# Split weight tiles 16 bytes later in their rooms: activations stand 48 in place of 64 bytes off them modulo 128

## The chip, the cores and the metric

The kernel runs on one core of one Trainium2 chip. Its time is the device time of one execution, in microseconds; three runs of the kernel before gave 1188.04, 1191.52 and 1197.49 us. The profile is of one further execution.

## The reference

Three transformer layers on one sequence of 256 tokens with a width of 1024, all in float32. Each `@` below is a matrix product with weights that are read once from memory.

```python
# layer 0
x = x + conformer_conv(rms_norm(x), w_pw1 [1024x2048], w_dw [31 taps], w_pw2 [1024x1024])
x = x + memory_cross_attention(rms_norm(x), mem, w_q, w_k, w_v, w_o)      # each 1024x1024
x = x + (silu(h @ w_gate) * (h @ w_up)) @ w_down      # h = rms_norm(x), 1024x2816, 2816x1024
# layer 1
k, v = shared_kv(x, w_k, w_v)
x = x + diff_attention(rms_norm(x), k, v, w_q, w_o)
x = x + memory_cross_attention(...)
x = x + swiglu(...)                                   # 1024x2816 twice, 2816x1024
x = rms_norm(x)
# last layer (hybrid)
proj = rms_norm(x) @ w_in                             # 1024x1816
o = three NSA branches and a sliding window attention on proj
x = x + rms_norm(o @ w_out)                           # 1024x1024
x = x + rms_norm(gated_conv_ffn(rms_norm(x), w_up [1024x5632], conv of width 3, w_down [2816x1024]))
```

## The kernel before, in words

**Tiles.** All weights are cut into tiles of 1024 x 256 (8 chunks of 128 rows, 256 columns), 1 MB each, in the order in which the stages use them. The activations lie transposed in on-chip memory: 128 partitions, and for each chunk of 128 features one row of 256 tokens (`Hhi`, `Hlo`, `FH`, `FL`, `KVr` and others, float32).

**Splitting.** Most products are made from split operands. A weight tile arrives by DMA in `raw[j]` (j is 0 or 1, two buffers in turn). ACT copies it in two halves to `whi[j]`, which has the shorter type float32r (`split`, lines 1004 and 1007); DVE then takes `raw[j] - whi[j]` and writes it to `wlo[j]`, the low part (`lower`, lines 1451 and 1456). The activations are split in the same way into a high and a low tensor. For each chunk the function `three` issues three matmuls into the same sum: high by high (line 491), low activations by high weights (492), high activations by low weights (493). Each matmul has its own weight load, which the profile shows as PEld, and which runs while the matmul before it streams.

**Turned and not.** In `matmul(dst, w, x)` the first operand, 128 columns, is loaded into the array, and the second, 256 columns, is streamed. Mostly the loaded one is a slice of `whi` or `wlo` and the streamed one a chunk of activations. In a few stages, turned ones, it is the reverse: activations are loaded and `whi` or `wlo` streamed, so that the result has the tokens on the partitions. Among them are the values of the attention (`diffv`), the last part of the input projection, the output projection `wout` and the last down projection `down2`. The profile's names list the streamed operand first: `acc<-Hhi,whi` streams `Hhi` and loads `whi`, `acc<-whi,FH` streams `whi` and loads `FH`.

**Order.** Every engine has its program written out by hand, and semaphores link them. A tile's chain is: SP issues the load of `raw[j]` once `wlo[j]` of the tile before in this buffer is written (`lo_dve`); ACT waits for the load and for the matmuls of the tile two before (`tile_done`); DVE waits for ACT; PE waits for DVE (`tile_in`), and for a free accumulator (`acc_free`). Between the splits ACT and DVE do the elementwise work of the stage. Memory keys and values (`memk`, `memv`, `memk1`) are made from `raw` directly in full float32, without a split (lines 507 and 527). In `wout` the four weight tiles have places of their own (`out_weights`): the first two use `whi` and `wlo`, the third `Hhi` and `Hlo`, the fourth parts of `KVr`.

**Places.** `sb` allocates on-chip memory from the front, one tensor after the other; a tensor's bytes are those of one partition. `raw`, `whi` and `wlo` are three pairs of 8192 bytes. Behind them lies `apart`, which nothing reads or writes: 176 x 4 = 704 bytes, or 5 x 128 + 64. Everything from `X` on to the constants `cst` (`Hhi`, `Hlo`, `H2`, `MEM`, `FH`, `FL`, `KVr`, `MKV`, `A`) has a size that is a multiple of 1024 bytes, and chunks of 1024 bytes. By this order of allocation `raw`, `whi` and `wlo` stand at 0 modulo 128 and all the activations at 64 modulo 128; every slice that a matmul takes of them starts at a multiple of 512 bytes from the tensor's start. `Hhi` and `FH`, and `KVr` and `FH`, which meet in `wout`, stand 0 apart modulo 128.

Of the kernel before, what the change touches and what calls it, by code (L numbers as in the profile page):

```python
# [7 lines left out]
F32R = mybir.dt.float32r  # L8
# [8 lines left out]
P = 128  # L17
# [6 lines left out]
KC = 8  # L24
MB = 256
# [134 lines left out]
def build(nc, weights, consts, x_in, mem_in, positions, out):  # L160
    ctx = ExitStack()
    with ctx:
        def sb(name, shape, dt=F32, where=ctx):
            return where.enter_context(nc.sbuf_tensor(name, shape, dt))
# [3 lines left out]


        raw = [sb(f"raw{j}", [P, KC, MB]) for j in range(2)]  # L170
        whi = [sb(f"whi{j}", [P, KC, MB], F32R) for j in range(2)]
        wlo = [sb(f"wlo{j}", [P, KC, MB], F32R) for j in range(2)]
        sb("apart", [P, 176])
        X = sb("X", [P, DC, S])
        SQ = sb("SQ", [P, DC, S])
# [2243 lines left out]
```

## Time and profile before

| what | us |
|---|---|
| median of three runs | 1191.52 |
| lowest and highest | 1188.04, 1197.49 |
| the profiled execution's own time | 1196.01 |
| its span, first to last instruction | 1194.2 |
| PE busy (matmuls) | 1144.7 |
| PE weight loads busy | 1088.0 |
| DVE busy | 876.8 |
| ACT busy | 612.3 |
| POOL busy | 64.3 |
| read from memory | 194.12 MB |

PE is the matmul engine, PEld its weight load, which overlaps with the matmuls; DVE and ACT are the two elementwise engines; SP issues most DMAs. The matmuls are pipelined: one lasts nearly 300 ns in the records, but the next starts long before it ends, so several are in flight, and a matmul's cost is the distance from one start to the next. A count of instructions in a window takes in those that were already running at its left edge. The mean granted clock of TensorE is 0.99 of full speed. Some rows stand in a window, given as start:end in us from the start of the span.

### The profile page before, as it was taken

What the parts mean: (1) busy time and instruction counts of PE and PEld (TensorE: products, weight loads), DVE (VectorE), ACT (ScalarE), POOL (GpSimd) and SP (SyncE); (2) the same over time, 40 slices, a digit from 0 to 9 for tenths busy, and PEclk for the clock granted to TensorE, in tenths of its full rate; (3) what the DMA queues carried; (4) which work ended last, traced back from release to release, by engine and by line L of the source; (5) the groups of instructions that cost most, each with busy time, mean ns of one, the idle gap of its engine ahead of it and who ended that gap; (6) DMA issues with size and microseconds to landing.
All of it is one profiled execution on the core that took longest, in us unless ns stands there. A gap on an engine that the chain in (4) does not pass through costs nothing.

```text
span 1194.2 us, 24046 instructions
## 1 busy us (share of the span) xinstructions
PE 1144.7 (96%) x9142; PEld 1088.0 (91%) x9142; DVE 876.8 (73%) x1480; ACT 612.3 (51%) x1072; POOL 64.3 (5%) x53
## 2 busy tenths in 40 slices
PE   9999999999999999998999999999979799999997
PEld 8988898999999999778989999999967599999997
DVE  6999886676666687556768666657897857999954
ACT  6754555544445544344445444454455745666542
POOL 0677000000000000000000000000000000000000
PEclk9999999999999999999999999999989989999999
DMA  8554443355555656124524555565553213455562
GB/s 286 177 189 164 141 162 121 128 191 190 196 188 199 212 188 226 63 72 162 207 70 170 189 189 195 177 212 196 210 181 107 71 41 124 172 183 198 181 212 106
DMA packets 32008, 198.42 MB, mean 166 GB/s; under 512 B 3776, under 2 KB 6080, under 8 KB 9024
## 3 DMA queue, kind: packets, MB, share of 16 engines
q1 hardware_dynamic: 29440, 193.09, 46.8%
q10 hardware_dynamic: 2496, 4.33, 1.1%
q8 instruction: 51, 0.84, 0.3%
q14 instruction: 21, 0.17, 0.0%
HBM read 194.12 MB, written 1.05 MB: 163 GB/s over the span
## 4 chain that ended last, share of the span: by engine, by line
PE 74%; DVE 17%; ACT 3%; issue 3%; DMA 1%; ACTq 0%; DVEq 0%; SPq 0%
PE acc L491 21%; PE acc L492 20%; PE acc L493 20%; DVE sc L1923 4%; PE acc L507 2%; DVE wlo L1456 2%; PE acc L774 2%; DMA raw<-weights 1%; PE acc L527 1%; DVE wlo L1451 1%; PE sc L738 1%; PE st L642 1%; PE tp L763 1%; ACT whi L1004 1%; DVE mx L1833 1%
## 5 line engine op out<-in xcount | busy, mean ns | idle before, releaser
L491 PE MATMUL acc<-Hhi,whi 128*128 128x256 f32 x1368 | 384.3, 281 | 5.3 <-DVE wlo L1456 5.2
L492 PE MATMUL acc<-Hlo,whi 128*128 128x256 f32 x1368 | 381.1, 279 | 0.0
L493 PE MATMUL acc<-Hhi,wlo 128*128 128x256 f32 x1368 | 381.1, 279 | 0.0
L1004 ACT ACTIVATE whi<-raw 128x1024 fp32r<-128x1024 f32 x160 | 169.4, 1059 | 335.1 <-PE acc L493 304.3
L1451 DVE TENSOR_TENSOR wlo<-raw,whi 128x1024 fp32r<-128x1024 f32 (+1 forms) x158 | 193.6, 1225 | 106.0 <-ACT whi L1004 105.6
L491 PEld LDWEIGHTS acc<-Hhi,whi 128*128 128x128 f32 x1368 | 257.8, 188 | 7.6 <-DVE wlo L1456 4.4
L493 PEld LDWEIGHTS acc<-Hhi,wlo 128*128 128x128 f32 x1368 | 258.7, 189 | 0.0
L492 PEld LDWEIGHTS acc<-Hlo,whi 128*128 128x128 f32 x1368 | 256.8, 188 | 0.2
L1456 DVE TENSOR_TENSOR wlo<-raw,whi 128x1024 fp32r<-128x1024 f32 (+1 forms) x158 | 193.3, 1223 | 1.6 <-ACT whi L1007 0.3
L491 PE MATMUL acc<-FH,whi 128*128 128x256 f32 x608 | 170.6, 281 | 5.2 <-DVE FH L2086 3.3
L493 PE MATMUL acc<-FH,wlo 128*128 128x256 f32 x608 | 169.5, 279 | 0.0
L1007 ACT ACTIVATE whi<-raw 128x1024 fp32r<-128x1024 f32 x160 | 167.2, 1045 | 0.0
L491 PEld LDWEIGHTS acc<-FH,whi 128*128 128x128 f32 x608 | 115.2, 189 | 6.8 <-issue 3.5
L493 PEld LDWEIGHTS acc<-FH,wlo 128*128 128x128 f32 x608 | 115.4, 190 | 0.0
L492 PE MATMUL acc<-FL,whi 128*128 128x256 f32 x352 | 98.0, 279 | 0.0
L492 PE MATMUL acc<-FH,whi 128*128 128x256 f32 x256 | 71.6, 280 | 0.0
L492 PEld LDWEIGHTS acc<-FL,whi 128*128 128x128 f32 x352 | 66.1, 188 | 0.0
L491 PE MATMUL acc<-whi,FH 128*128 128x256 f32 (+1 forms) x186 | 53.4, 287 | 6.7 <-DVE TG L2157 4.5
L1923 DVE SCALAR_TENSOR_TENSOR sc<-A,cst,sc 128x256 f32<-128x256 f32 x136 | 54.5, 481 | 0.1
L492 PE MATMUL acc<-wlo,FH 128*128 128x256 f32 (+1 forms) x186 | 53.3, 287 | 0.0
L1223 ACT ACTIVATE E<-sc,nb 128x256 f32<-128x256 f32 (+1 forms) x64 | 27.2, 429 | 46.4 <-DVE nb L1842 38.4
L492 PEld LDWEIGHTS acc<-FH,whi 128*128 128x128 f32 x256 | 48.8, 191 | 0.0
(356 smaller groups left out, 2007.5 us busy)
## 6 DMA issues: line engine op xcount, KB each, us to landing
raw<-weights SPq DMA_DIRECT2D x177, 1024.0 KB, 4.9
MEM<-mem_in SPq DMA_DIRECT2D x2, 1024.0 KB, 7.3
held<-weights SPq DMA_DIRECT2D x2, 1024.0 KB, 5.9
E<-A ACTq DMA_DIRECT2D x12, 128.0 KB, 2.4
X<-x_in ACTq DMA_DIRECT2D x4, 256.0 KB, 6.1
raw<-weights SPq DMA_DIRECT2D x4, 256.0 KB, 6.9
MEM<-consts ACTq DMA_DIRECT2D x2, 512.0 KB, 4.9
out<-MKV SPq DMA_DIRECT2D x4, 256.0 KB, 2.1
```

The lines of the kernel that those rows point to most:

```text
L491: pe.matmul(dst, w, x, start=first, stop=False)
L492: pe.matmul(dst, w, xl, start=False, stop=False)
L493: return pe.matmul(dst, wl, x, start=False, stop=last)
L507: mm = pe.matmul(acc[1][:, m, :], raw[k % 2][:, c, m * P:(m + 1) * P], MEM[:, c, :], start=c == 0, stop=c == KC - 1)
L527: mm = pe.matmul(acc[j][:, m, :], x[:, o] if turned else w[:, o], w if turned else x, start=c == 0, stop=c == KC - 1)
L774: mm = pe.matmul(dst[rows, c0:c0 + w], v, PT[0:kn, n % 2, p0:p0 + pw], start=first, stop=last)
L1004: act.activation(whi[j][:, 0:HALF, 0:width], raw[j][:, 0:HALF, 0:width], ACT.Copy).then_inc(hi_out, 1)
L1007: act.activation(whi[j][:, HALF:KC, 0:width], raw[j][:, HALF:KC, 0:width], ACT.Copy).then_inc(hi_out, 1)
L1223: ins = act.activation(E[:, n % 3, m, 0:u["keys"]], sc[:, 2 * (n % 2) + m, 0:u["keys"]], ACT.Exp, bias=nb[:, n % 2, m:m + 1], scale=u["sca ...
L1451: dve.tensor_tensor(out=wlo[j][:, 0:HALF, n], in0=raw[j][:, 0:HALF, n], in1=f(whi[j][:, 0:HALF, n]), op=ALU.subtract)
L1456: dve.tensor_tensor(out=wlo[j][:, HALF:KC, n], in0=raw[j][:, HALF:KC, n], in1=f(whi[j][:, HALF:KC, n]), op=ALU.subtract).then_inc(lo_dve, 1)
L1923: ins = dve.scalar_tensor_tensor(out=tap_sums[k], in0=src, scalar=w, in1=tap_sums[k], op0=ALU.mult, op1=ALU.add)
```

## The change

The four tensors `whi[0]`, `whi[1]`, `wlo[0]` and `wlo[1]` become views into rooms that are 32 elements (128 bytes) longer, and each view starts 4 elements (16 bytes) behind the start of its room. The view has the shape of the tile before, and everything that uses it is the same. `raw` in front of them stays where it is. What lies behind moves by 4 x 128 = 512 bytes, so it keeps its place modulo 128. `whi` and `wlo` stand at 16 modulo 128, and the activations 48 bytes behind them modulo 128; seen from the activations, the weights are 80 bytes on.

```diff
--- before.py
+++ after.py
@@ -168,8 +168,9 @@
 
 
         raw = [sb(f"raw{j}", [P, KC, MB]) for j in range(2)]
-        whi = [sb(f"whi{j}", [P, KC, MB], F32R) for j in range(2)]
-        wlo = [sb(f"wlo{j}", [P, KC, MB], F32R) for j in range(2)]
+        inside = lambda t: t[:, 4:4 + KC * MB].rearrange("p (k m) -> p k m", k=KC)
+        whi = [inside(sb(f"whi{j}", [P, KC * MB + 32], F32R)) for j in range(2)]
+        wlo = [inside(sb(f"wlo{j}", [P, KC * MB + 32], F32R)) for j in range(2)]
         sb("apart", [P, 176])
         X = sb("X", [P, DC, S])
         SQ = sb("SQ", [P, DC, S])
```

## Rows read from the trace of the kernel before

**Rows 1.** The page, first line and busy time of each engine over the span.
```profile
span 1194.2 us, 24046 instructions
PE 1144.7 (96%) x9142; PEld 1088.0 (91%) x9142; DVE 876.8 (73%) x1480; ACT 612.3 (51%) x1072; POOL 64.3 (5%) x53
```

**Rows 2.** The page, chain of waits, shares of the span by engine and line.
```profile
PE 74%; DVE 17%; ACT 3%; issue 3%; DMA 1%; ACTq 0%; DVEq 0%; SPq 0%
PE acc L491 21%; PE acc L492 20%; PE acc L493 20%; DVE sc L1923 4%; PE acc L507 2%; DVE wlo L1456 2%; PE acc L774 2%; DMA raw<-weights 1%; PE acc L527 1%; DVE wlo L1451 1%; PE sc L738 1%; PE st L642 1%; PE tp L763 1%; ACT whi L1004 1%; DVE mx L1833 1%
```

**Rows 3.** Who waited for whom: us in total, times, longest.
```profile
ACT whi L1004 <- PE acc L493: 304.3, 118, 5.5
PE acc L491 <- DVE wlo L1456: 10.0, 9, 2.2
```

**Rows 4.** Busy time (and instructions) of each engine in two windows of the gate/up stages.
```profile
core 0: us, PE busy (x) PEld busy (x) DVE busy (x) ACT busy (x) POOL busy (x), PEclk, DMA share, GB/s
300.00:340.00 40.00, 40.00 (x356) 40.00 (x355) 27.32 (x31) 18.24 (x22) 0.00 (x0) 1.00 0.54 184
700.00:740.00 40.00, 40.00 (x342) 40.00 (x341) 26.00 (x29) 18.66 (x23) 0.00 (x0) 1.00 0.54 188
```

**Rows 5.** Groups of instructions in these two windows, first 300:340, then 700:740.
```profile
L491 PE MATMUL acc<-Hhi,whi 128*128 128x256 f32 x119 | 32.8, 276 | 0.0
...
L491 PE MATMUL acc<-Hhi,whi 128*128 128x256 f32 x114 | 32.0, 281 | 0.0
```

**Rows 6.** Groups over the span, shapes kept apart: xcount, busy us, mean ns, idle before.
```profile
L493 PE MATMUL acc<-Hhi,wlo 128*128 128x256 f32 x1368 | 381.1, 279 | 0.0
```

**Rows 7.** Timeline, PE alone, output projection: start us, us; five left out.
```profile
982.71 0.28 PE L493 MATMUL acc<-Hhi,FH 128*128 128x256 f32 x1
...
983.43 0.28 PE L493 MATMUL acc<-Hhi,FH 128*128 128x256 f32 x1
```

**Rows 8.** Groups in 982.4:987.3, output projection of the last layer.
```profile
L491 PE MATMUL acc<-KVr,FH 128*128 128x256 f32 x8 | 2.3, 283 | 0.0
```

**Rows 9.** Around 975.5, one streamed column: timeline, then group (mean ns).
```profile
974.89 1.25 PE L665 MATMUL st<-ones,SQ 128*128 128x1 f32 x10
...
L665 PE MATMUL st<-ones,SQ 128*128 128x1 f32 x10 | 1.3, 250 | 0.0
```

**Rows 10.** The page, the groups that split a weight tile.
```profile
L1004 ACT ACTIVATE whi<-raw 128x1024 fp32r<-128x1024 f32 x160 | 169.4, 1059 | 335.1 <-PE acc L493 304.3
L1451 DVE TENSOR_TENSOR wlo<-raw,whi 128x1024 fp32r<-128x1024 f32 (+1 forms) x158 | 193.6, 1225 | 106.0 <-ACT whi L1004 105.6
L1456 DVE TENSOR_TENSOR wlo<-raw,whi 128x1024 fp32r<-128x1024 f32 (+1 forms) x158 | 193.3, 1223 | 1.6 <-ACT whi L1007 0.3
L1007 ACT ACTIVATE whi<-raw 128x1024 fp32r<-128x1024 f32 x160 | 167.2, 1045 | 0.0
```

**Rows 11.** Busy time in a window of the last up stage.
```profile
1022.00:1118.00 96.00, 95.85 (x816) 94.85 (x816) 90.70 (x145) 60.22 (x92) 0.00 (x0) 1.00 0.54 186
```

**Rows 12.** Groups over the span, the other forms of line 491.
```profile
L491 PE MATMUL acc<-FH,whi 128*128 128x256 f32 x608 | 170.6, 281 | 5.2 <-DVE FH L2086 3.3 <-DVE wlo L1456 1.3 <-DVE FH L2013 0.6
L491 PE MATMUL tp<-Hhi,whi 128*128 128x256 f32 x128 | 36.3, 283 | 2.5 <-DVE Hlo L1494 1.3 <-DVE H L1494 0.6 <-DVE wlo L1895 0.5
L491 PE MATMUL acc<-H,whi 128*128 128x256 f32 x64 | 17.8, 278 | 0.1
L491 PE MATMUL acc<-whi,FH 128*128 128x256 f32 x154 | 43.0, 279 | 0.0
L491 PE MATMUL acc<-whi,Hhi 128*128 128x256 f32 x80 | 22.7, 284 | 1.3 <-DVE wlo L1456 1.3
L491 PE MATMUL sc<-whi,FH 128*128 128x256 f32 x38 | 10.7, 282 | 0.0
```

**Rows 13.** Timeline of matmuls, then of weight loads, around 400.3 us.
```profile
400.22 0.28 PE L492 MATMUL acc<-FL,whi 128*128 128x256 f32 x1
...
400.23 0.19 PEld L493 LDWEIGHTS acc<-FH,wlo 128*128 128x128 f32 x1
```

## The prediction

> **What bounds the kernel now.** I read the engine shares first: PE is busy 96% of the span, DVE 73%, ACT 51% [rows 1]. Then the chain of waits: 61% of the span lies on three lines, 491 to 493, the three matmuls by which a float32 product is made from split operands; DVE has 17% [rows 2]. The waits say the same from the other side: ACT, which makes the next split tile, waits 304.3 us in total for PE, and PE waits 10.0 us in total for the split tile [rows 3]. So the time is set by how far apart the starts of consecutive matmuls of these lines lie (their pitch), and the reader should look for nothing else first.
>
> The pitch is not one number. In a stretch of the first gate/up stage 356 matmuls overlap a window of 40 us; in the same stage of the second layer, same lines, shapes, tiles and granted clock (1.00), it is 342 [rows 4]. About three of each count were already in flight at the window's edge (one lasts 276 ns, 113 apart), so the pitches are 40/353 = 113.3 ns and 40/339 = 118.0 ns. The mean durations go with them, 276 and 281 ns [rows 5], so the means of a line tell how often each pitch was had: line 493 on Hhi has 381.1 us in 1368, or 278.6 ns [rows 6], midway. I call these the short and the long pitch. A stage keeps one of them through dozens of tiles, past every tile boundary. Nothing else in the rows distinguishes them: DMA share 0.54 in both, DVE 27.3 and 26.0 us, ACT 18.2 and 18.7 us [rows 4].
>
> Is this memory placement at all? One stage lets that be seen. In the output projection of the last layer the weight tile is once `whi` (64 bytes off the activations modulo 128, by the order of allocation) and once `Hhi` or `KVr` (0 off). With 0 off, six pitches take 983.43 - 982.71 = 0.72 us, 120.0 ns each [rows 7], at a mean duration of 283 ns [rows 8]: a third pitch, which I find in no steady stretch of the tiles that are 64 off. And matmuls that stream a single column, so that only the weight load can limit them, are ten in 1.25 us from the first start to the last end; one lasts 0.25, so nine pitches take 1.00 us, 110 to 112 ns each within the rounding [rows 9]. That is the nearest row to a floor for anything that loads 128 columns of float32 each time. I take 111.5. So at 64 off a matmul costs 1.8 or 6.5 ns over this floor and at 0 off 8.5 ns.
>
> The Trainium skill, "TensorE: Matmul & The Clock Gate", section "Step-by-step: what each phase is for", says that the array has two independent read ports, so that loading the next weights takes no read bandwidth from the running matmul; placement would then be worth nothing and the sum would be 0. The 120.0 against 113.3 ns of the rows, with the same instruction in the same shape, speak against it as a whole truth, though they can't say that 16 bytes matter.
>
> **The change, part by part.** No instruction, wait, transfer or loop is added, removed or moved. Three things alter.
>
> (a) The rooms are 128 bytes longer. 4 x 128 = 512 bytes more of a partition, and every tile behind them moves by a multiple of 128, so nothing but `whi` and `wlo` changes its place modulo 128. I cost this at nothing; no instruction's size depends on it.
>
> (b) ACT writes `whi` and DVE reads it and writes `wlo` 16 bytes later. These take 1059 and 1045 ns (ACT) and 1225 and 1223 ns (DVE) each [rows 10]. No row shows them at another place. Bounds: below, nothing; above, what hides them. ACT waits 304.3 us for PE, so even 10% more on its 336.6 us is covered. DVE stands idle for 40.00 - 27.32 = 12.7 us of a 40 us window of the gate/up stage [rows 4]; only in the last up stage is it near its limit, 90.70 of 96.00 us [rows 11]. If that cover went, 1% more for DVE there would be 0.9 us. I take 0. The transfers land in `raw`, which stays.
>
> (c) PE reads weights and activations 48 instead of 64 bytes apart. This is the whole change. It concerns the rows of line 491 with `whi` [rows 6, 12]: unturned (weights loaded, activations streamed) 1368 + 608 + 128 + 64 = 2168, turned (activations loaded, weights streamed) 154 + 80 + 38 = 272; times three, 6504 and 816, together 7320. One nanosecond of pitch is worth 7.3 us, 0.6% of the time.
>
> No row shows 48. Bounds by the nearest rows: the floor, 111.5 ns, and the pitch at 0 off, 120 ns. The mean now is 115.7 (half of 113.3, half of 118.0). So the ends are -4.2 x 7320 = -31 us and +4.3 x 7320 = +31 us. In distance, 48 is nearer to 64 (113.3 and 118.0) than to 0. Which way inside that? The weight load for the next matmul is recorded to start with, or 10 ns behind, the running matmul: 400.22 for the matmul and 400.23 for the load [rows 13]. The matmul streams 1024 bytes in a pitch of 113 ns, 9 bytes per ns, so a lag of 3 or 4 ns (an estimate, from starts that agree to within 10 ns) puts the two readers not 64 but some 64 + 30 bytes apart while they run. If 64 apart in flight is best, as 0 off being worst suggests, an unturned pair should gain from a smaller distance of addresses, and 48 is a step that way; a turned pair, whose distance becomes 80, should lose by as much. I therefore take for the unturned the middle of floor and short pitch, 112.5 ns: 6504 x 3.2 = 20.8 us less. For the turned ones, which mostly have the long pitch in the rows (279, 284 and 282 ns against 276) [rows 12], I take a step to the pitch at 0 off at worst, 816 x 2 = 1.6 us more, half of it: 0.8.
>
> What is late next: the split tiles. In the last up stage DVE leaves PE 5.3 us in 96 [rows 11], and 816 matmuls there would gain 2.6 us, which fits, though not all of it at the boundaries where PE waits for DVE; in the first stage, before 60 us, PE waits for the split already. I take off 2.5 us. Sum: -20.8 + 0.8 + 2.5 = -17.5 us.
>
> The profiled execution took 1196.0 us, of which 1194.2 are the span [rows 1]; it is 4.5 us over the median of 1191.52. Part of that may be that it had more stretches at the long pitch than the median run: one long stage of 1,200 matmuls at the other pitch is 5.6 us, and the three runs shown lie 9.5 us apart. From the profiled one the sum gives 1178.5, from the median 1174.0. I take 1176.
>
> **The forecast (45%).** The unturned matmuls run at 111.5 to 113.3 ns almost everywhere. Its ends: everything just at the short pitch, half of 7320 by 4.7 = 17 less 2 hidden, from 1196.0: 1181; everything at the floor, 31 less 4, from the median: 1165. Own range 1164 to 1183.
>
> **Rival 1, no difference (27%).** Two pitches remain, with about the shares of today, or one pitch near 115 takes their place: a shift of 16 bytes is 1.7 ns of streaming, and lengthening the short pitch by it while the long one disappears gives 115.0, 0.7 below the mean, -5 us. Time 1186 to 1197. For it: the pitch seems to be chosen anew whenever a burst of matmuls starts, not by an address, since both are had at one and the same placement. It includes the case that the change doesn't do what it says, because the placement modulo 128 that I read from the order of allocation isn't the one the chip has. The skill's rule on two ports leads here too. Against it: 120.0 against 113.3.
>
> **Rival 2, slower (28%).** The distance that counts is the one of addresses, 64 is the middle between two collisions, and 48 is a step towards the 120 ns of 0 off. Then the short pitch can't be held and every stretch runs at 118: the other half of 7320 by 4.7, +17 us, 1208 from the median; at 120, +31 us, 1223. It decides from a mean pitch of 117.3 on, where the loss passes 1%. For it: 0 off is worst, and an optimum found between 0 and 128 by symmetry is 64. Against it: the lag of the load, and that in distance 48 is three quarters of the way.
>
> **How the numbers follow.** 1% of this time, 12 us, is about what a measurement of this kernel can tell from no change. Faster by more than that is the forecast, 0.45; within it rival 1, 0.27; slower rival 2, 0.28. The range for 8 in 10 reaches from the floor, 1164, to everything at the long pitch, 1209; left out are the 120 ns end of rival 2 (about 0.1) and gains below the floor with the tails (less than 0.1).
>
> **What the changed profile would show.** Right: counts of 355 to 362 matmuls in a 40 us window of both gate/up stages, a mean of line 491 on Hhi of 276 ns or less, and the turned stretch after 1130 us no faster. No difference: counts of 342 in one stage and 356 in the other, whichever, or near 351 in both. Slower: 342 or fewer everywhere, or 283 ns as with `KVr`. ACT and DVE rows of the splits that differ by more than 2% would show that (b) was not free. The prediction fails at once if the loads and matmuls show one pitch that doesn't depend on the 16 bytes; its weakest step is the sign, taken from the lag.

## The result and the profile after

The changed kernel takes 1210.12 us in the median of four runs (1208.41 to 1211.35); the kernel before, run beside it on the same chip, 1192.08. The ratio is 1.0147, with an interval of 1.0116 to 1.0179: slower. The forecast was 1176; of the three cases the second rival, slower with about 1208, comes nearest. The profiled execution took 1210.4 us, 1208.6 of them the span, at a mean granted clock of 0.983.

The page of the changed kernel (its lines are numbered one higher: 492 to 494 are the three split matmuls): span, busy time, the chain's shares by engine, then three groups of the costliest, with count, busy us and mean ns.

```profile
span 1208.6 us, 24046 instructions
...
PE 1164.3 (96%) x9142; PEld 1106.7 (92%) x9142; DVE 875.9 (72%) x1480; ACT 611.7 (51%) x1072; POOL 63.2 (5%) x53
...
PE 84%; DVE 9%; ACT 3%; issue 2%; DMA 2%; ACTq 0%; DVEq 0%; SPq 0%
...
L1005 ACT ACTIVATE whi<-raw 128x1024 fp32r<-128x1024 f32 x160 | 169.4, 1059 | 347.9 <-PE acc L494 315.0
L1452 DVE TENSOR_TENSOR wlo<-raw,whi 128x1024 fp32r<-128x1024 f32 (+1 forms) x158 | 193.3, 1223 | 112.0 <-ACT whi L1005 111.3
...
L1457 DVE TENSOR_TENSOR wlo<-raw,whi 128x1024 fp32r<-128x1024 f32 (+1 forms) x158 | 193.3, 1223 | 1.6 <-ACT whi L1008 0.3
```

Same instructions, same count. The span has grown by 14.4 us and PE's busy time by 19.6, DVE's and ACT's not at all: against [rows 1]. The splits take what they took, 1059 and 1223 ns against 1059 and 1225 [rows 10]; ACT waits for PE 10.7 us longer than in [rows 3]. The chain has moved from DVE to PE, 84% and 9% against 74% and 17% [rows 2]. So PE alone became slower, and the others wait for it.

Busy time (and instructions) in the windows of [rows 4, 11]:

```profile
300.00:340.00 40.00, 40.00 (x343) 40.00 (x342) 26.09 (x29) 17.20 (x20) 0.00 (x0) 1.00 0.53 184
700.00:740.00 40.00, 40.00 (x342) 40.00 (x342) 25.89 (x29) 18.75 (x24) 0.00 (x0) 1.00 0.55 189
1022.00:1118.00 96.00, 94.39 (x799) 94.19 (x798) 90.52 (x146) 61.71 (x96) 0.00 (x0) 1.00 0.52 181
```

343 and 342 where it was 356 and 342, at the same granted clock of 1.00; 799 for 816 in the last up stage. The counts look like the long pitch everywhere. They aren't. The timeline, PE alone, gives single starts (start us, us); between the first and the second line lie 42 pitches, and 42 between the third and the fourth:

```profile
268.03 0.28 PE L492 MATMUL acc<-Hhi,whi 128*128 128x256 f32 x1
...
273.02 0.28 PE L492 MATMUL acc<-Hhi,whi 128*128 128x256 f32 x1
...
273.74 0.28 PE L492 MATMUL acc<-Hhi,whi 128*128 128x256 f32 x1
...
278.64 0.28 PE L492 MATMUL acc<-Hhi,whi 128*128 128x256 f32 x1
```

4.99 / 42 = 118.8 ns in one weight tile, 4.90 / 42 = 116.7 ns in the next (43 matmuls of the 48 of a tile each), and so on in turn through every gate/up stage. These are two new pitches, and they change with the tile, that is with the buffer, where those of before held for the whole of the first two gate/up stages and for stretches of ten tiles or so in the last (118 ns from 1072 to 1104 us, 113 before and behind). Nowhere is there a stretch at 113.3. What no one changed kept its pitch: the matmuls that stream `KVr`, 0 off, have their mean duration of 283 ns of [rows 8] still, and their starts lie 120.0 ns apart as before.

```profile
L492 PE MATMUL acc<-KVr,FH 128*128 128x256 f32 x8 | 2.3, 283 | 0.0
```

**Which buffer is which.** The allocation in the built program answers it. `raw` and, behind it, the room of `whi[0]` start at 128 modulo 256, the activations stand at 64, and a room of 2048 + 32 elements is 8320 bytes, 32.5 times 256. So the first buffer of each kind has its weights at 144 and the second at 16 modulo 256. From here on I give the distance as streamed operand less loaded operand, modulo 256. For an unturned matmul it was 192 in both buffers before; after, it is 64 - 144 = 176 in the one and 64 - 16 = 48 in the other. The change made two placements, and only one of them is the "48" of its name.

### The profile page after: what moved, and what is told of

The parts are those of the page before. It is cut to its first block, busy times and chain, and to the rows that moved or that the text cites. A ratio compares the mean times of both kernels' runs of the same rounds, so it can differ in the third digit from the quotient of the medians.

```text
span 1208.6 us, 24046 instructions
## 1 busy us (share of the span) xinstructions
PE 1164.3 (96%) x9142; PEld 1106.7 (92%) x9142; DVE 875.9 (72%) x1480; ACT 611.7 (51%) x1072; POOL 63.2 (5%) x53
## 4 chain that ended last, share of the span: by engine, by line
PE 84%; DVE 9%; ACT 3%; issue 2%; DMA 2%; ACTq 0%; DVEq 0%; SPq 0%
PE acc L492 21%; PE acc L494 21%; PE acc L493 21%; PE acc L528 7%; PE acc L508 2%; PE acc L775 2%; DMA raw<-weights 2%; DVE wlo L1457 1%; DVE wlo L1452 1%; PE sc L739 1%; PE tp L492 1%; PE tp L493 1%; PE tp L494 1%; PE acc L712 1%; PE st L643 1%
## 5 line engine op out<-in xcount | busy, mean ns | idle before, releaser
L1005 ACT ACTIVATE whi<-raw 128x1024 fp32r<-128x1024 f32 x160 | 169.4, 1059 | 347.9 <-PE acc L494 315.0
L1452 DVE TENSOR_TENSOR wlo<-raw,whi 128x1024 fp32r<-128x1024 f32 (+1 forms) x158 | 193.3, 1223 | 112.0 <-ACT whi L1005 111.3
L1457 DVE TENSOR_TENSOR wlo<-raw,whi 128x1024 fp32r<-128x1024 f32 (+1 forms) x158 | 193.3, 1223 | 1.6 <-ACT whi L1008 0.3
L1008 ACT ACTIVATE whi<-raw 128x1024 fp32r<-128x1024 f32 x160 | 167.3, 1045 | 0.0
```

The source lines that it names most:

```text
L1005: act.activation(whi[j][:, 0:HALF, 0:width], raw[j][:, 0:HALF, 0:width], ACT.Copy).then_inc(hi_out, 1)
L1008: act.activation(whi[j][:, HALF:KC, 0:width], raw[j][:, HALF:KC, 0:width], ACT.Copy).then_inc(hi_out, 1)
L1452: dve.tensor_tensor(out=wlo[j][:, 0:HALF, n], in0=raw[j][:, 0:HALF, n], in1=f(whi[j][:, 0:HALF, n]), op=ALU.subtract)
L1457: dve.tensor_tensor(out=wlo[j][:, HALF:KC, n], in0=raw[j][:, HALF:KC, n], in1=f(whi[j][:, HALF:KC, n]), op=ALU.subtract).then_inc(lo_dve, 1)
```

## The experiments

Two theories at first. A: the pitch is set by the two operands' places modulo 256, each pair with its own; the 16 bytes chose worse ones. B: the distance modulo 128 counts, and the room's length or something that moved behind it plays a part. C, added on the way: the sign of a shift decides, as the lag of the forecast had it. For every kernel I take the mean pitch M of the split matmuls from the starts in its trace (some 7,350 pairs of consecutive starts, about 6,400 unturned). Where one draws the line between a pitch and a wait moves M by up to 0.1 ns, in all kernels alike. The kernels were timed on different chips, each beside the kernel before; so the ratio is what compares them, not the time.

**map_places**: a kernel of its own, which has bursts of 96 of the split matmuls and nothing beside them, with the activations at 16 places of 16 bytes' step and the weights at 128.

```
room = sb(NAMES[i], [P, 1024 + 64], F32R)
o = STEP // 4 * i    # STEP is 16
places.append(room[:, o:o + 1024].rearrange("p (k s) -> p k s", k=4))
```

> A kernel of its own, no part of the reference: it leaves out the whole computation and only times matmuls of the split kind. Weights at one fixed place, 16 activation tensors (a to p) that stand 0, 16, 32, ... 240 bytes off them modulo 256, for each a burst of 96 matmuls (weights loaded, activations streamed) and one turned (activations loaded, weights streamed), three times over with different pauses between. Nothing else runs. Theory A, the place modulo 256 sets the pitch: the curve over the 16 places differs between d and d + 128, is near 116.7 ns at 48 and near 118.7 ns at 176, and has 113.3 or 117.8 at 192 (the two pitches of before), 120 at 0. Theory B, the place modulo 128 alone: places 128 apart give the same pitch, and 48 and 176 about 117.7 both. Theory C, the pitch is no matter of places but of what the other engines do: all 16 places give one pitch here. The lag argument of the prediction asks for a minimum at 32 or 48 for the unturned and at 80 or 96 for the turned.

Three pairs of its timeline, PE alone, each 30 pitches apart at the end of a burst: `h` is 112 off, `a` 0, `m` 192.

```profile
203.91 0.28 PE L87 MATMUL acc<-h,wlo 128*128 128x256 f32 x1
...
207.31 0.28 PE L87 MATMUL acc<-h,wlo 128*128 128x256 f32 x1
...
421.70 0.28 PE L87 MATMUL acc<-a,wlo 128*128 128x256 f32 x1
...
425.30 0.28 PE L87 MATMUL acc<-a,wlo 128*128 128x256 f32 x1
...
1127.70 0.28 PE L87 MATMUL acc<-m,wlo 128*128 128x256 f32 x1
...
1131.23 0.28 PE L87 MATMUL acc<-m,wlo 128*128 128x256 f32 x1
```

3.40, 3.60 and 3.53 us: 113.3, 120.0 and 117.7 ns, with no other engine's work beside them and next to no transfer (3 GB/s at most). Read in the same way for all (unturned, ns, last 30 pitches of the bursts): 0 off 120.0; 16 and 128 to 160, 118.7; 32, 116.7 or 117.8; 48, 118.3; 64, 117.8; 80, 118.2 or 120.0; 96, 120.0; 112, 113.3 three times of three; 176, 119.2; 208, 118.9 to 119.2; 192, 113.3 twice and 117.8 once; 224, 118.3; 240, 117.1. It is no curve: the neighbours of the two good places lie 5 to 7 ns above them. And 192, the place of before, has two pitches with nothing else in the kernel, only other pauses ahead of its three bursts. Theory B falls here: places 128 apart differ (112 off has 113.3 and 240 off 117.1). So does the lag, by which the lowest pitch should have been at 32 or 48 off: they have 116.7 to 118.3 ns, and the lowest are at 112 and 192.

**rooms_only**: the changed kernel with its longer rooms, but the tiles at their start.

```
-        inside = lambda t: t[:, 4:4 + KC * MB]...     # the rest of the line is cut here
+        inside = lambda t: t[:, 0:0 + KC * MB]...
```

> The changed kernel with the longer rooms (8320 bytes in place of 8192) but no shift of 16 bytes. Modulo 128 everything stands as in the kernel before; modulo 256 the activations stand 192 bytes off the first buffer and 64 off the second, where before it was 192 for both. Theory B (modulo 128 alone, the 16 bytes did it all): 1188 to 1197 us, pitches of 113.3 and 117.8 ns as before. Theory A (modulo 256): a pitch that changes with every second tile, and a time that differs from before by more than 0.5%, of either sign; if the rooms did the whole loss, 1210 us.

Measured 1192.20 us, ratio 1.0008 (0.9992 to 1.0024). Windows 300 to 340 and 700 to 740:

```profile
300.00:340.00 40.00, 40.00 (x356) 40.00 (x355) 27.36 (x30) 19.14 (x24) 0.00 (x0) 1.00 0.58 198
700.00:740.00 40.00, 40.00 (x355) 40.00 (x355) 27.29 (x30) 17.93 (x22) 0.00 (x0) 1.00 0.53 184
```

Both stages happened to have the short pitch; others of the same trace have 117.8, M is 114.7. The length of the room alone costs nothing, although its second buffer is 64 off and not 192. This is what theory B expected and not what A did: A holds only if 64 and 192 off have the same two pitches, 113.3 and 117.8, as the maps then show. What costs is the 16 bytes.

**shift_only**: the shift, in rooms of 33 times 256 bytes, so that both buffers are 176 off.

```
-        whi = [inside(sb(f"whi{j}", [P, KC * MB + 32], F32R)) ...   # wlo likewise
+        whi = [inside(sb(f"whi{j}", [P, KC * MB + 64], F32R)) ...
```

> The shift of 16 bytes alone, in rooms 256 bytes longer, so that both buffers stand alike modulo 256: activations 176 bytes off the weights modulo 256 (48 modulo 128) for both. Theory B: the time of the changed kernel, 1210 us, since the place modulo 128 is the same. Theory A: in the changed kernel the even tiles (176 off) have 118.7 ns and the odd ones (48 off) 116.7 ns; now all should have 118.7 ns, 7300 times half of 2 ns or 7 us more than the changed kernel, about 1217 us.

Measured 1215.09 us, ratio 1.0200 (1.0161 to 1.0239), a little worse than the changed kernel.

```profile
300.00:340.00 40.00, 40.00 (x339) 40.00 (x338) 25.67 (x29) 17.25 (x21) 0.00 (x0) 1.00 0.53 184
700.00:740.00 40.00, 40.00 (x339) 40.00 (x339) 25.71 (x29) 18.28 (x22) 0.00 (x0) 1.00 0.54 184
```

339 in both windows, 118.7 ns in every unturned tile that is split into `whi` and `wlo`, without alternation. That is the slower half of the changed kernel, made whole.

**map_512**: the first map with 32 places, up to 496 bytes, in bursts of 48.

> The map of places again, no part of the reference, with 32 places 16 bytes apart (0 to 496 modulo 512; a to p, then aq to pq) and bursts of 48 matmuls. In the first map the 16 places modulo 256 lay 0 or 256 further on modulo 512 by turns. Theory A (modulo 256): places 256 apart have one pitch, and at 48, 112, 192 the unturned have 118.3, 113.3 and 113.3 or 117.8 again. Theory D (a wider pattern than 256): they differ, and 48 is 116.7 while 304 is 118.3, which would also explain why the changed kernel's odd tiles, with one operand at 48 and one at 304 modulo 512, had 116.7.

Places 256 bytes apart had the same pitches in every one of the three rounds, 118.3 ns for 48 and 304 off among them. Theory A's modulus stands, and B's 128 falls once more: 48 and 176 off differ. At 192 off it also answers part of what the first map left: ahead of a burst of 113.3 the pause was 752 ns there and 984 here, ahead of one of 117.8 it was 986 there and 749 here. So the length of the pause doesn't decide which pitch follows.

**both_48**: both buffers 48 off, in one long room for two tiles (the two lines that they replace, and the ends of the new ones, are left out).

```
+        rooms = [sb(n, [P, 2 * KC * MB + 128], F32R) for n in ("whi", "wlo")]
+        whi, wlo = ([t[:, 4 + j * KC * MB:4 + (j + 1) * KC * MB]... for j in range(2)] for t in rooms)
-        sb("apart", [P, 176])
+        sb("apart", [P, 16])
```

> The four split tiles in two rooms, so that both buffers, high and low, stand alike modulo 512, and all activations 48 bytes off them modulo 512. If the odd tiles of the changed kernel (48 off modulo 256, 116.7 ns) tell the pitch: 6400 x 1.4 = 9 us and 1 for the turned over before, 1202 us. If the map's pitch at 48 does (118.3 ns): 19 + 1 us, 1212. By theory B (modulo 128 alone): 117.7, 1210, as the changed kernel.

```profile
300.00:340.00 40.00, 40.00 (x345) 40.00 (x344) 25.79 (x29) 17.41 (x21) 0.00 (x0) 1.00 0.54 187
700.00:740.00 40.00, 40.00 (x345) 40.00 (x344) 26.32 (x30) 17.21 (x20) 0.00 (x0) 1.00 0.53 184
```

Measured 1205.37 us, ratio 1.0076 (1.0044 to 1.0109); 116.7 ns in every unturned tile, 119.1 in the turned ones, which are 208 off. With `shift_only` it takes the changed kernel apart: halfway between their ratios, 1.0076 and 1.0200, lies 1.0138, and the changed kernel has 1.0147. (The times fit better still, 1210.23 against 1210.12, but on different chips that is luck.) But the map had 118.3 at 48 off, so the distance isn't all.

**both_112**: the same with `sb("apart", [P, 32])`, 112 off, the map's best place.

> The same rooms, activations 112 bytes off the split weights. The map had 113.3 ns there for the unturned in all three bursts, and 120 for the turned. If places alone set the pitch: 6400 x (115.3 - 113.3) = -13 us, 950 x (120 - 117.1) = +3 us, less 1 that PE must wait for DVE: 1183 us, a ratio of 0.992. If the short pitch is a matter of how a burst starts and not of the place, both pitches appear and the time is 1192. Rival of the prediction (lag): a minimum below 64, so 112 would be slower than before, over 1200.

```profile
300.00:340.00 40.00, 40.00 (x336) 40.00 (x335) 25.26 (x29) 17.91 (x22) 0.00 (x0) 1.00 0.54 184
```

A miss: 1216.22 us, ratio 1.0174 (1.0127 to 1.0221), 120.0 ns where the map has 113.3 at the same distance. Not quite everywhere: of some 270 unturned blocks of 24 matmuls, about 30 have 116.7 or 118.3 ns, between 213 and 236 us and between 565 and 588 us from the start among them. What differs is where the pair stands: weights at 144 here, at 128 in the map.

**map_pairs**: 16 places of the weights (16 bytes' step) with 8 of the activations (32 bytes' step), all pairs, bursts of 48.

```
weights = [(at("w" + NAMES[i], 16 * i), at("v" + NAMES[i], 16 * i)) for i in range(16)]
places = [at("x" + NAMES[i], 32 * i) for i in range(8)]
```

> No part of the reference: bursts of 48 split matmuls for 16 places of the weight tiles (128 + 16 j modulo 256, tensors wa to wp for high and va to vp for low) against 8 of the activations (128 + 32 i, xa to xh), unturned and turned. In the two maps before, the weights stood at 128 and only the activations moved; the kernel that stood 112 apart by moving the weights to 144 had 120.0 ns where the map had 113.3, and the one 48 apart had 116.7 where the map had 118.3. Theory E, the pair of places counts and not the distance alone: of pairs with one distance those whose weights stand at an odd multiple of 16 differ from the others; w 144 with x 0 (112 apart) gives 120, w 144 with x 192 (48 apart) 116.7, w 128 with x 64 (192 apart) 113.3 or 117.8. Theory F, the distance counts and the kernel's other engines or its chunk order make the rest: every pair of one distance gives the map's value, 112 apart 113.3 and 48 apart 118.3. By either, 113.3 ns is the shortest pitch found, and there should be pairs that have it at any start.

Its timeline around one place of the weights, `wf`/`vf`, an odd multiple of 16; again 30 pitches from line to line of a pair. `xe` is 48 off, `xg` 112, and in the last pair, turned, `wf` is streamed past a loaded `xh`, also 112 off, but the loaded operand stands at an even multiple of 16.

```profile
610.28 0.28 PE L83 MATMUL acc<-xe,vf 128*128 128x256 f32 x1
...
613.78 0.28 PE L83 MATMUL acc<-xe,vf 128*128 128x256 f32 x1
...
636.00 0.28 PE L83 MATMUL acc<-xg,vf 128*128 128x256 f32 x1
...
639.60 0.28 PE L83 MATMUL acc<-xg,vf 128*128 128x256 f32 x1
...
655.40 0.28 PE L79 MATMUL acc<-wf,xh 128*128 128x256 f32 x1
...
658.80 0.28 PE L79 MATMUL acc<-wf,xh 128*128 128x256 f32 x1
```

116.7, 120.0 and 113.3 ns. I put the bursts of all three maps together (544, either 17 or 34 to a cell) by the distance and by whether the loaded operand's place is an even or odd multiple of 16 bytes (steady pitch in ns; a comma parts pitches that were both had; a dash: no such pair was run):

| off | even | odd | off | even | odd |
|---|---|---|---|---|---|
| 0 | 120.0 | - | 128 | 118.7 | - |
| 16 | 118.7, 113.3, 116.7 | 120.0, 117.3 | 144 | 118.7, 116.7 | 120.0 |
| 32 | 116.7, 117.8 | - | 160 | 118.7, 117.3 | - |
| 48 | 118.3 | 116.7 | 176 | 119.2 | 118.7 |
| 64 | 117.8, 113.3 | - | 192 | 113.3, 117.8 | - |
| 80 | 118.3, 120.0 | 118.1 | 208 | 119.0, 116.6 | 117.8, 118.3, 123.3 |
| 96 | 120.0 | - | 224 | 118.3 | - |
| 112 | 113.3 | 120.0 | 240 | 117.1 | 118.3 |

A cell holds unturned and turned bursts and those of three kernels, and where it has one value they agree to 0.3 ns (without the very first burst of `map_512`, which starts at 213 ns a matmul): turning is no case of its own, it exchanges which operand is loaded. The table accounts for every kernel so far: before 192 even, the changed one 176 and 48 odd, 116.7 in `both_48` against 118.3 in the first map, and the 120.0 of `both_112`, 112 odd. It is not complete: the 116.7 and 118.3 that `both_112` also had are in none of the 17 bursts of that cell. And it was made after these kernels; what it is worth as a forecast the next three show.

**both_64**: the kernel before with `sb("apart", [P, 144])`, so that both are 64 off and not 192.

> The kernel before with one number changed: apart has 144 elements in place of 176, so all activations stand 64 bytes off the split weights modulo 256 in place of 192 (64 modulo 128 in both). Map of pairs: turned at 64 has 113.3 ns in 8 of 8 pairs (192: 117.8 in 8 of 8), unturned 113.3 in 6 of 8 (192: 2 of 8; 3 of 6 in the first two maps, where 64 had 117.8 in all 6). If the map's turned pitch holds: 950 x (117.1 - 113.5) = -3.4 us; if unturned goes from half at 113.3 to three quarters: 6400 x 1.1 = -7 us more; together 1182 us, a ratio of 0.991. If the unturned get the 117.8 of the first maps: -3 + 16, 1204 us. If modulo 128 is what counts: 1192.

```profile
300.00:340.00 40.00, 40.00 (x342) 40.00 (x341) 25.59 (x28) 17.22 (x20) 0.00 (x0) 1.00 0.55 186
700.00:740.00 40.00, 40.00 (x355) 40.00 (x354) 26.47 (x30) 17.21 (x20) 0.00 (x0) 1.00 0.56 186
```

Measured 1204.36 us (1194.77 to 1210.53), ratio 1.0091 (1.0056 to 1.0126). That is one of the three times expected, 1204, but not for the reason given there, all unturned at 117.8 and the turned at 113.5: the trace has neither. It has the two pitches of before, 113.3 and 117.8, the long one oftener: in blocks of 24 consecutive split matmuls, 208 of the trace have the long pitch and 97 the short one, where before it was 145 and 153. Its ten runs lie 16 us apart. One placement thus doesn't fix the time; how often each pitch is caught does. Nor do the maps tell how often: the turned matmuls here are 192 off, where the maps had 113.3 in 15 of 17 turned bursts, and they ran at 117.2 in the mean, against 117.5 in the kernel before.

**w_earlier**: the shift the other way. The rooms of `both_48` with 60 in place of 4 and `apart` 48 elements: weights at 112, both 208 off.

> The shift in the other direction: split weights 16 bytes earlier (112 modulo 256), activations where they were (64), so 208 apart modulo 256, 80 modulo 128, both buffers alike. Map of pairs at 208: unturned 117.8 in 7 of 8, turned 118.3: 6400 x 2.5 + 950 x 1.2 = 17 us more than before, 1209 us. The lag argument, had only its sign been wrong, wants this side to be the better one: under 1188 us. A symmetric optimum at 64 modulo 128 wants the same loss as for 16 bytes later in like rooms (shift_only): 1215.

```profile
300.00:340.00 40.00, 40.00 (x327) 40.00 (x326) 25.18 (x28) 17.84 (x22) 0.00 (x0) 1.00 0.50 174
700.00:740.00 40.00, 40.00 (x327) 40.00 (x326) 25.54 (x28) 18.23 (x22) 0.00 (x0) 1.00 0.51 180
```

Measured 1223.03 us (1218.06 to 1231.48), ratio 1.0241 (1.0190 to 1.0292): the slowest of all, above its forecast. Here single starts lie 116.7 and 130 ns apart in turn, 123.3 in the mean, in long stretches, and 117.8 in others, two of the values of 208 odd in the table; which of them the kernel would keep I had not reckoned with. Theory C falls with it: a shift of 16 bytes loses in both directions, and had only the sign of the lag been wrong, this side should have come in under 1188 us.

**x_later**: the weights at 128 as before, the split activations moved instead, to 240: 112 off with the weights even, where the map has 113.3 unturned each time.

```
-        sb("apart", [P, 176])
+        sb("apart", [P, 24])
+        def later(name, n, where):
+            return sb(name, [P, n * S + 64], F32R, where)[:, 4:4 + n * S]...
```

(`Hhi`, `Hlo`, `H2`, `FH` and `FL` are made with it; these lines, and three fillings of 256 bytes, are left out.) With the shorter `apart` everything else behind it moves too, from 64 to 224 modulo 256, and ACT and DVE have 20 more instructions on their registers.

> The weights as in the kernel before (128 modulo 256), and the split activations (Hhi, Hlo, H2, FH, FL) moved to 240 modulo 256 by rooms of their own and a shorter apart: 112 apart, with the weights at an even multiple of 16. The maps had 113.3 ns for the unturned there in 9 of 9 bursts, where moving the weights instead (both_112) had 120.0. The turned had 120 in the maps. If the pair of places decides: unturned 6400 x (115.3 - 113.3) = -13 us, turned 950 x (120 - 117.1) = +3, less 1 that PE must wait for DVE: 1182 us with a small spread, a ratio of 0.992. If the distance alone decided, as in both_112: 1216. If in the kernel the starts of bursts bring other pitches than the maps show: between these.

```profile
300.00:340.00 40.00, 40.00 (x356) 40.00 (x355) 27.23 (x30) 18.30 (x22) 0.00 (x0) 1.00 0.52 184
700.00:740.00 40.00, 40.00 (x355) 40.00 (x354) 27.50 (x31) 18.39 (x23) 0.00 (x0) 1.00 0.54 187
```

The pitch came as the table says: 113.3 in every stage, unturned mean 113.6; the turned matmuls, 144 off with the loaded operand odd, went from 117.5 to 120.0, the table's value too. The time did not: 1191.85 us, ratio 1.0010 (0.9994 to 1.0026), where 1182 was expected. Its page has the chain, and its waits tell what PE waits for (us, times, longest):

```profile
PE 65%; DVE 21%; ACT 5%; issue 5%; DMA 2%; DVEq 1%; ACTq 1%; SPq 0%
```

```profile
PE acc L498 <- DVE wlo L1463: 12.3, 12, 2.3
```

PE has 65% of the chain against 74% [rows 2]; it waits 12.3 us for the split tile against 10.0 [rows 3]. Its M is 1.15 ns under that of before, 8.5 us in 7350, and its span only 4.7 us shorter: 3.8 us came back beside the matmuls, by waits or by what else moved; no run parts the two. The rest of what was expected was probably never there to be had, though this is argued and not shown: the profiled execution of before lay some 4.5 us over the median, so that the median run will have a smaller M. `rooms_only`, next to that median, has 114.7.

**All kernels on one line.** M by the span of the same execution:

| kernel | off, mod 256 (buffers) | M, ns | span, us | span - 7350 M |
|---|---|---|---|---|
| x_later | 112 | 114.4 | 1189.5 | 348.9 |
| rooms_only | 192, 64 | 114.7 | 1191.2 | 347.9 |
| before | 192 | 115.5 | 1194.2 | 345.1 |
| both_64 | 64 | 116.3 | 1197.3 | 342.2 |
| both_48 | 48 | 116.9 | 1205.2 | 345.7 |
| after | 176, 48 | 117.8 | 1208.6 | 342.8 |
| shift_only | 176 | 118.7 | 1212.2 | 340.0 |
| both_112 | 112 (loaded odd) | 119.4 | 1214.9 | 337.4 |
| w_earlier | 208 | 121.3 | 1229.7 | 338.0 |

From the first to the last, 40.2 us for 6.95 ns: 5.8 us of span for one ns of pitch, where the matmuls alone would make 7.35. The last column shows where the rest is: on the whole, the longer the pitch, the less time stands beside it. The order by M is the order by span, without exception. Two other kinds of matmul in these nine traces don't answer to the places: those in full float32 of the same shape (`acc<-raw,MEM`, not split) start 215.8 ns apart in all nine, though `MEM` moved against `raw` in four of them, and the turned split matmuls that stream 152 columns in place of 256 start 111.6 to 111.7 ns apart in all nine, at the floor of [rows 9].

## Why the prediction was wrong

**What bounds the kernel** was right. Nine kernels that differ in places alone, but for 20 register instructions in `x_later`, are in the order of their pitch, over 40 us of span. The maps show the pitch to depend on the two operands' places with nothing else at work and, at some places, on something that changes from burst to burst.

**(b), the splits at nothing**, was right: 1059, 1045 and 1223 ns as before. ACT and DVE don't feel these 16 bytes.

**(a), "every tile behind them moves by a multiple of 128 ... I cost this at nothing"**, was wrong as a model and right as a price for the room alone (`rooms_only`, 1.0008). The modulus is 256, and the room of 32.5 times 256 bytes put the two buffers at different places. With the shift, this is worth the difference between `shift_only` and the changed kernel: it made the loss smaller, a ratio of 1.0147 in place of 1.0200.

**(c), the sign from the lag**, is the step that failed. The forecast put the unturned matmuls at 112.5 ns, by an argument from the distance. It assumed that the distance acts smoothly, that 64 modulo 128 is one placement, and that a weight load which trails by a few ns moves the best distance to one side. None of it holds. In place of 112.5 the changed kernel has 118.7 in one buffer and 116.7 in the other. 64 and 192 off are two placements; both neighbours of the old one lose (`shift_only` 1.0200, `w_earlier` 1.0241); and on the first map, a step of 16 bytes from 112 or 192 off leads to between 118.7 and 120.0. "In distance, 48 is nearer to 64 than to 0" was the wrong way to choose between the bounds. The bounds themselves, 111.5 and 120 ns, held for all but `w_earlier`, and none of the kernels came under 113.3, so the floor from the one-column row wasn't reached. The forecast's -20.8 us was a gain of 3.2 ns; the unturned mean went from 115.3 to 117.7, +2.4 ns, or 6504 x 2.4 = +15.6 us. The turned term, +0.8, was +1.1 (816 x 1.4 ns, from 117.5 to 118.9). Together 16.7, of which the span shows 14.4; the other 2.3 us are probably hidden beside waits, which fits the chain's smaller share of DVE but was not tried by itself. The medians lie 18.0 apart, since the profiled execution of before was above its median and that of the changed kernel at it.

**Rival 2** had the time, 1208, by its own price: the short pitch can't be held, and 118 follows. The price was right and the mechanism only half. The short pitch is indeed gone; what takes its place is not the long one but 118.7 in one buffer and 116.7 in the other, whose mean, 117.7, is a hair from 117.8 by chance. Its reason, that 64 modulo 128 is the best because it is the middle, holds in the look of it only: seen from 192 off, both neighbours are indeed slower. But the two placements that are 64 modulo 128 differ, since `both_64` loses 0.9%, and the one pair of places that had 113.3 in every burst is 112 off, 16 bytes from the 128 off that by symmetry is as bad as 0. `x_later`, which has it, is as fast as the kernel before.

**Rival 1** reckoned with a pitch chosen when a burst starts. That was right for before, rooms_only and both_64, where 113.3 and 117.8 are both had at one placement; it is not what the change met.

The Trainium skill's rule on two read ports ("TensorE: Matmul & The Clock Gate", section "Step-by-step: what each phase is for"), by which a load takes nothing from the running matmul, would have every place of the maps alike. They lie from 113.3 to 123.3 ns, by where the loaded operand stands to the streamed one. So this case's runs decide against it for split operands of 256 columns; what the two reads share, no run shows.

**What stays open.** Why a pair of places has the pitch it has, the maps don't say; they are a table and not a mechanism. Why the same pair holds 113.3 in one burst and 117.8 in the next is open too. It is settled in the first few matmuls of a burst, `m` in the first map has its pitch from the sixth distance on at the latest, but the length of the pause before doesn't decide it, and I could name no condition that does.

## What to carry to other kernels

Where one engine's instructions follow each other without a gap, take the pitch between starts from the timeline before anything else: 0.05 us over 40 of them is 1%, and no busy share shows it. When operands' places are touched, write down every tensor's place modulo 256, each buffer's by itself; a room that isn't a multiple of 256 bytes makes a second placement. And don't interpolate between two measured placements: measure the pair in a small kernel of bursts, turned and unturned apart, and then ask what the faster pitch will wait for.

## What the runs showed of the hardware

- The pitch of 128 x 128 by 256 float32 split matmuls, each with its own load, depends on the operands' places modulo 256, and differs from one step of 16 bytes to the next: from 113.3 ns (112 off, loaded operand even) to 120.0 (0 off; 112 off, odd) and 123.3 (208 off, odd), at a granted clock of 1.00, which is the upper level, 2.4 GHz.
- Some pitches are even and some are means of a pattern: at 113.3, 117.8 and 120.0 single starts lie within 1 or 2 ns of the mean distance (`before`, `both_112`), at 208 off they are 116.7 and 130 ns apart in turn (`w_earlier`), and after the change they run through a pattern of 115 to 121.
- A placement can hold two pitches (113.3 and 117.8 at 64 and at 192 off), each for hundreds of matmuls, and take its pick anew after a pause. The ten runs of `both_64` lie 16 us apart and the seventeen of before on one chip too; but the ten of `rooms_only`, which has both pitches, lie 4 us apart, and the ten of `both_48`, which has one, 9 us, so the spread alone doesn't tell the two kinds apart.
- ACT and DVE, which write and read the same tiles in turn, did not answer to the place: the two subtractions took 1218 to 1227 ns in all nine kernels of the table, the first copy on ACT 1059 to 1062.
- The same places leave two other kinds of matmul alone: those in full float32 (`acc<-raw,MEM`) keep 215.8 ns from start to start, and split ones that stream 152 columns keep 111.6 to 111.7, in all nine kernels.
